# Feed-forward entry by token blocks, and the down products of its last two steps by token block

## The reference, cut to what matters

```python
for l in range(DEPTH):                      # DEPTH = 2
    x = x + token_mixer(rmsnorm(x, ln1_g[l]), ...)
    h = rmsnorm(x, ln2_g[l])
    if l % 2 == 0:
        x = x + (jax.nn.silu(h @ w_gate) * (h @ w_up)) @ w_down   # 1024 -> 2816 -> 1024
    else:
        x = x + moe(h, ...)
return rmsnorm(x, final_g)
```

## Time and profile before

| | |
|---|---|
| median of 3 runs | 1437.19 us (1436.74 to 1437.25) |
| the profiled execution | 1435.53 us, span of the trace 1433.7 us |
| PE busy | 1411.7 us, 98% of the span |
| DVE, ACT, POOL busy | 438.5, 303.6, 135.2 us |
| mean granted TensorE clock | 0.996 of 2.4 GHz |
| chain that ended last | PE 96%, DVE 2%, issue 1%, DMA 1% |

### The profile page before, as it was taken

How to read it: one execution, slowest core, us unless ns; L and a number is a source line. 1 busy time by engine, 2 the same in 40 slices (tenths; PEclk the granted TensorE clock), 3 DMA queues, 4 the chain that set the end, 5 groups by cost and what they waited for, 6 DMA issues and landing times.

```text
span 1433.7 us, 35214 instructions
## 1 busy us (share of the span) xinstructions
PE 1411.7 (98%) x16271; PEld 890.3 (62%) x16271; DVE 438.5 (31%) x719; ACT 303.6 (21%) x426; POOL 135.2 (9%) x164
## 2 busy tenths in 40 slices
PE   9999999999999999999999999999999999999996
PEld 7999999999999984344344344344344344344344
DVE  5775765555776563110110110110110110110122
ACT  5554454444646431000000000000000000000001
POOL 2650000000363000000000000000000000000000
PEclk9999999999999999999999999999999999999999
DMA  9755555666366455999999999999999999999993
GB/s 318 254 177 177 177 167 191 200 214 202 125 208 204 170 194 219 417 420 418 410 420 413 413 421 410 413 420 410 415 419 408 414 421 407 416 420 410 420 421 159
DMA packets 136220, 462.72 MB, mean 323 GB/s; under 512 B 8515, under 2 KB 74849, under 8 KB 121746
## 3 DMA queue, kind: packets, MB, share of 16 engines
q1 hardware_dynamic: 130498, 449.94, 80.8%
q0 software_dynamic: 2448, 7.90, 1.5%
q10 hardware_dynamic: 3136, 2.75, 0.6%
HBM read 455.70 MB, written 4.86 MB: 321 GB/s over the span
## 4 chain that ended last, share of the span: by engine, by line
PE 96%; DVE 2%; issue 1%; DMA 1%; ACT 0%; SPq 0%; POOLq 0%; DVEq 0%; POOL 0%
PE bank L1425 94%; PE bank L1575 1%; DMA mem<-in_w_in_dram 1%; PE bank L1455 0%; DVE w_lo L740 0%; DVE mem L788 0%; DVE mem L782 0%; ACT mem L537 0%; DVE mem L1006 0%; DVE x L804 0%; PE bank L1669 0%; PE bank L1543 0%; PE bank L1606 0%; DVE xt_lo L795 0%; DVE x L1212 0%
## 5 line engine op out<-in xcount | busy, mean ns | idle before, releaser
L1425 PE MATMUL bank<-mem 128*32 128x448 f32 (+2 forms) x11632 | 876.0, 463 | 0.9 <-DVE mem L1219 0.6
L1425 PEld LDWEIGHTS bank<-mem 128*32 128x32 f32 (+1 forms) x11632 | 381.0, 110 | 495.1 <-issue 377.3
L740 DVE TENSOR_TENSOR w_lo<-mem,w_hi 128x1024 fp32r<-128x1024 f32 x178 | 223.1, 1270 | 127.4 <-ACT w_hi L514 126.5
L1265 DVE TENSOR_TENSOR mem<-mem,bank 128x448 f32<-128x448 f32 x48 | 26.9, 616 | 726.1 <-PE bank L1425 726.1
L1425 PE MATMUL bank<-xt_hi,w_hi 128*128 128x256 f32 x864 | 238.8, 276 | 0.0
L1425 PE MATMUL bank<-xt_hi,w_lo 128*128 128x256 f32 x864 | 237.6, 275 | 0.0
L1425 PE MATMUL bank<-xt_lo,w_hi 128*128 128x256 f32 x864 | 237.6, 275 | 0.0
L514 ACT CAST w_hi<-mem 128x1024 fp32r<-128x1024 f32 x178 | 184.4, 1048 | 173.3 <-PE bank L1425 167.9
L1425 PEld LDWEIGHTS bank<-xt_hi,w_hi 128*128 128x128 f32 x864 | 165.8, 192 | 1.3 <-issue 0.7
L1425 PEld LDWEIGHTS bank<-xt_lo,w_hi 128*128 128x128 f32 x864 | 165.8, 192 | 0.3
L1425 PEld LDWEIGHTS bank<-xt_hi,w_lo 128*128 128x128 f32 x864 | 165.9, 192 | 0.0
(11 more groups left out here) (206 smaller groups left out, 722.5 us busy)
## 6 DMA issues: line engine op xcount, KB each, us to landing
mem<-in_eg_dram SPq DMA_DIRECT2D x128, 896.0 KB, 11.0
mem<-in_eu_dram SPq DMA_DIRECT2D x128, 896.0 KB, 10.8
mem<-in_ed_dram SPq DMA_DIRECT2D x112, 1024.0 KB, 13.1
mem<-in_w_in_dram SPq DMA_DIRECT2D x40, 1024.0 KB, 6.4
mem<-in_fg_dram SPq DMA_DIRECT2D x11, 1024.0 KB, 5.3
mem<-in_fu_dram SPq DMA_DIRECT2D x11, 1024.0 KB, 5.3
mem<-in_fd_dram SPq DMA_DIRECT2D x11, 1024.0 KB, 4.9
mem<-in_w_br_dram SPq DMA_DIRECT2D x8, 1024.0 KB, 5.1
```

What stands on the lines that cost most here:

```text
L740: nc.vector.tensor_tensor(w_lo[:, q % H, :], src, w_hi[:, q % H, :].bitcast(F32), ALU.subtract).then_inc(lo_done, 1)
L1265: nc.vector.tensor_tensor(h, h, by_pair(bank[3 + g]), ALU.mult).then_inc(ehf_done, 1)
L1425: return nc.tensor.matmul(out, lhs, rhs, start=first, stop=last, skip_group_check=True)
```

## The change

At the entry, PE computes step 0's gate and up by token block: the normalised tokens become the stationary operand, the weights the moving one, 24 products of 256 columns for each of gate and up and each block (`first_pass`). Gate of block 0 comes ahead of block 1's transposes. Of the 12 zero products 3 stay. The hidden values of step 0 come out with tokens in rows, so four transposes turn them (`first_hidden_turned`) between gate and up of step 1; ACT and DVE work on halves of 256 columns for step 0. On ACT and DVE pieces 60 and 61 are split after the block's last norm operations, piece 59 ahead of them.

At the exit, PE takes the down products of steps 9 and 10 after the gate and up of step 10: block 0 of step 9, block 0 of step 10, then block 1 of both. `y_full` counts each output half. The calls of `until` behind the loop name a number smaller by 2; the loops on ACT and DVE are as they were.

```diff
@@ ACT, feed-forward entry
-                    until(q0 + 2 + H)
-                    act.wait_ge(piece_used, q0 + 2)
-                    nc.scalar.activation(sg[:, :], bank[0][:, :], ACT.Silu).then_inc(sg_done, 1)
-                    until(q0 + 4 + H)
-                    act.wait_ge(hf_done, 1)
-                    nc.scalar.copy(fh_hi[:, 0, :, :], hf[:, 0, :].rearrange("p (k t) -> p k t", k=2)).then_inc(fh_h, 1)
+                    for t in range(TB):
+                        if t == 0:
+                            act.wait_ge(first_gate, 1)
+                        else:
+                            act.wait_ge(piece_used, q0 + 2)
+                        nc.scalar.activation(halves(sg[:, 256 * t:256 * t + 256].unsqueeze(1)),
+                                             unturned(bank[FIRST_BANK[t][0]][:, 0:256]), ACT.Silu).then_inc(first_sg, 1)
+                        until(q0 + 2 * t + 2 + H)
+                    act.wait_ge(first_turned, 1)
+                    nc.scalar.copy(by_block(fh_hi[:, 0, :, :]),
+                                   bank[3][:, :].rearrange("p (k t a) -> p k t a", k=2, t=TB)).then_inc(fh_h, 1)
                     with act.Fori(0, (STEPS - 1) // 2) as r:
...
                     cur[0] = q0 + 4 + 6 * (STEPS - 1) + H
-                    until(q0 + FFN_PIECES + H - 2)
+                    until(q0 + FFN_PIECES + H - 4)
@@ DVE, second layer's first norm
                         if p < 3:
-                            dve.wait_ge(y_full, 1 + (1, 1, 2)[p])
+                            dve.wait_ge(y_full, 2 + p)
@@ PE, feed-forward entry
                 transposes(2 * l + 1, 0, 1)
-                keep_warm(8, bank[UNIT_BANK["wo0"]])
-                transposes(2 * l + 1, 1, 0)
-                transposes(2 * l + 1, 1, 1)
-                keep_warm(4, bank[UNIT_BANK["wo0"]])
+                if l:
...
+                else:
+                    keep_warm(3, bank[UNIT_BANK["wo2"]])
...
+                    def first_pass(t, u):
+
+                        for half in range(2):
+                            pe.wait_ge(tl_done, 4 + 2 * t + half + 1)
+                            w = pair(piece(q0 + 2 * u + half), lambda a: a.rearrange("p (k n) -> p k n", k=4))
+                            for k in range(4):
+                                kk = 4 * half + k
+                                ins = mm3(bank[FIRST_BANK[t][u]][:, 0:256],
+                                          (xt_hi[:, kk, t * P:(t + 1) * P], xt_lo[:, kk, t * P:(t + 1) * P]),
+                                          pair(w, lambda a: turns(a[:, k, :])), kk == 0, kk == KT - 1)
...
-                    up(q0, (None,) * 4, None, ready=4)
+                    first_pass(0, 0)
+                    transposes(1, 1, 0)
+                    transposes(1, 1, 1)
+                    first_pass(0, 1)
+                    first_pass(1, 0)
+                    first_pass(1, 1)
@@ PE, feed-forward exit
-                    pe.wait_ge(fh_l, STEPS)
-                    w = [piece(q0 + FFN_PIECES - 2 + k) for k in range(2)]
                     for t in range(TB):
-                        for half in range(2):
-                            for k in range(2):
-                                ins = down_part(w[k], 0, k, t, half, k == 1)
...
+                        for step_of, s in ((STEPS - 1, 1), (STEPS, 0)):
+                            pe.wait_ge(fh_l, step_of)
+                            w = [piece(q0 + FFN_PIECES - 4 + 2 * (1 - s) + k) for k in range(2)]
+                            for half in range(2):
+                                for k in range(2):
+                                    ins = down_part(w[k], s, k, t, half, s == 0 and k == 1)
+                                    if (t, half) == (1, 1):
+                                        ins.then_inc(piece_used, 1)
+                                if s == 0 and (t, half) != (1, 1):
+                                    ins.then_inc(y_full, 1)
```

More of the change, by code:

```diff
@@ L1041, in _ @@
                 scaled(n, 3)
+                until(base + MIX_PIECES + H - 2)
                 turned_low(n, 2)
@@ L1061, in _ @@
                     q0 = FFN_BASE
-                    until(q0 + 4 + H)
-                    hidden(1, 0, q0 + 4)
+                    for t in range(TB):
+                        dve.wait_ge(first_sg, t + 1)
+                        if t == 0:
+                            dve.wait_ge(first_up, 1)
+                        else:
+                            dve.wait_ge(piece_used, q0 + 4)
+                        cols = slice(256 * t, 256 * t + 256)
+                        nc.vector.tensor_tensor(halves(hf[:, 0:1, cols]), halves(sg[:, cols].unsqueeze(1)),
+                                                unturned(bank[FIRST_BANK[t][1]][:, 0:256]), ALU.mult).then_inc(first_hf, 1)
+                        until(q0 + 2 * t + 2 + H)
+                    dve.wait_ge(first_hf, TB)
+                    dve.wait_ge(fh_h, 1)
+                    nc.vector.tensor_tensor(by_block(fh_lo[:, 0, :, :]),
+                                            bank[3][:, :].rearrange("p (k t a) -> p k t a", k=2, t=TB),
+                                            by_block(fh_hi[:, 0, :, :].bitcast(F32)), ALU.subtract).then_inc(fh_l, 1)
+                    dve.sem_inc(sg_done, 1)
+                    dve.sem_inc(hf_done, 1)
                     with dve.Fori(0, (STEPS - 1) // 2) as r:
@@ L1710, in _, with up @@
                 transposes(2 * l + 1, 0, 1)
[L1711 to L1714 removed]
+                if l:
+                    keep_warm(8, bank[UNIT_BANK["wo0"]])
+                    transposes(2 * l + 1, 1, 0)
+                    transposes(2 * l + 1, 1, 1)
+                    keep_warm(4, bank[UNIT_BANK["wo0"]])
+                else:
+                    keep_warm(3, bank[UNIT_BANK["wo2"]])
                 if l == 0:
                     q0 = FFN_BASE
[L1720 removed]
+                    def first_pass(t, u):
[7 more added lines that the diff above has]
+                                          pair(w, lambda a: turns(a[:, k, :])), kk == 0, kk == KT - 1)
+                            if t == TB - 1:
+                                ins.then_inc(piece_used, 1)
+                        if t == 0:
+                            ins.then_inc((first_gate, first_up)[u], 1)
+                        pe.wait_ge(lo_done, q0 + 2 * u + 2)
+                    def up(q, counts, free, between=None):
                         if free is not None:
                             pe.wait_ge(sg_done, free)
[L1724 removed]
+                        channels(bank[0], q, counts=counts[0:2])
+                        if between is not None:
+                            between()
                         if free is not None:
@@ L1748, in _ @@
                         mm(bank[4 + n][:, :], zeros[:, :], zeros[:, 0:1].to_broadcast([P, 512]), True)
-                    with pe.Fori(0, (STEPS - 1) // 2) as r:
+                    q = q0 + 4
+                    pe.wait_ge(first_sg, TB)
+                    up(q, (None,) * 4, None, first_hidden_turned)
+                    down(q + 4, 0, (None, None), 1)
+                    q = q0 + 10
+                    up(q, (None,) * 4, 2)
+                    down(q + 4, 1, (None, None), 2)
+                    with pe.Fori(1, (STEPS - 1) // 2 - 1) as r:
                         for s in range(2):
```

33 lines of the change are left out of this document (25 added, 8 removed).

## The result

The changed kernel took 1440.03 us (median of 14 runs, 1438.94 to 1440.44), the kernel before 1436.74 us (14 runs, 1435.01 to 1437.32) in the same comparison: a ratio of 1.0025 with a 95% interval of 1.0017 to 1.0033. It is 3.3 us slower; the forecast was +3.6 us and 1440.8 us, with a range of 1437.6 to 1443.4. The profiled execution took 1440.14 us with a span of 1438.3 us, against 1435.53 and 1433.7.

The account below looks back on a forecast made before the run. PE, busy 98% of the span, was taken to bound the kernel. Entry -2.9 and exit +4.7 make +1.8 us, with one clock fall +3.6, put on the median 1437.19: 1440.8 us, range 1437.6 to 1443.4.

Parts of the forecast that it names:

- Entry: Feed-forward entry on PE: step 1 starts 3.3 us earlier, four extra transposes cost 0.36 us; -2.9 us in all.
- The wait for step 10's hidden values: Exit on PE: after 12 instead of 24 step 9 down products, a new wait of 1.95 us, within the exit's +4.7.
- The adds behind two splits: Exit on DVE: first residual add behind splits of pieces 124 and 125, at 364.8 instead of 360.07; exit +4.7 us.
- The clock: Exit on PE: idle times of 1.95 and 2.8 us; one fall to half clock, taken at 1.8 us.
- What I set at nothing: No cost assumed for halved ACT and DVE work at entry, or elsewhere for the mixer's value products and pieces 126 and 127.
- D: Rival, 11%: exit loses nothing, first add 2.4 us or more before the last down product ends; -2.9 us, 1434.3.
- B: Rival, 25%: entry and exit as forecast but no fall of the clock; +1.8 us, 1439.0.
- C: Rival, 17%: a clock fall after each of the two exit gaps; +5.4 us, 1442.6.
- E: Rival, 7%: exit as forecast, no gain at the entry; +4.7 us, 1441.9, with a fall 1443.7.

Follow-up runs that it names:

- entry_only: The changed kernel with the down products of steps 9 and 10 as before the change: 1433.05 us, ratio 0.998, 2.9 us faster than the kernel before.
- hidden_first: splits_behind with step 10's hidden values ahead of piece 123 on ACT and DVE in the last turn: 1433.02 us, ratio 0.9981 to the kernel before.
- splits_behind: The full change with the last ACT and DVE loop turn written out, its last two splits behind block 0's norm: 1434.95 us, ratio 0.9995 to before.
- exit_only: The kernel before with only the new exit (down-product order and y_full counts): 1442.91 us, ratio 1.0047, 7.0 us slower than before.
- fill_gap: The full change with 18 zero products instead of 6 behind the last down product: 1438.71 us, ratio 1.0019 to the kernel before.
- norm_early: hidden_first with block 0 scaled ahead of adds 2 and 3, its transposes ahead of the last 6 down products, zeros and ACT moved: 1432.31 us, ratio 0.997.

## Why the prediction was right

- **Entry, forecast -2.9 us.** Right: 14.12 us instead of 17.37, and 0.36 for the extra transposes; entry_only measured -2.9. The gate's first product came after a wait of 0.29 us for the low part that `tl_done` counts. The halved operations on ACT and DVE stayed under step 1's gate products, as set: the transposes of the hidden values at 200.10 have no wait ahead of them.
- **The wait for step 10's hidden values, forecast 1.95 us.** Right: 24 less 12 products left no cover for a chain that is 4.5 us long. 353.58 is 1.93 us later than 12 products behind 349.06 allow. hidden_first shows which link was long: the cast and split of piece 123 ahead of the hidden product.
- **The adds behind two splits, forecast +4.7 us in all at the exit.** Right: the first add came 4.75 us later. The exit without the fall of the clock is 6.09 - 1.54 = 4.55 us, 0.2 less than the forecast's way gives. The forecast took the 6.17 us from the add to the mixer's product as all on the norm's chain; but before, the scaling stood behind the add that waited for the last product, 3.19 us behind the first add, and now it comes after 2.98. splits_behind and hidden_first took the two losses away one after the other: 1.0 and then 2.9 us below before. That the smaller bounds of `until` did nothing is seen in DVE's rows, where both splits (359.51) still stand ahead of the first add.
- **The clock, forecast one fall at 1.8 us.** Right in kind and place: one fall, behind the longer wait and not directly behind the wait of 1.77 us, in the full change and in exit_only. Its price was 1.5 us (fill_gap). The 1.8 came from the start of the kernel, 4.66 us for 24 products against 2.67, and that row holds more than the fall: in exit_only, whose start is the same code and had no fall, the 24 products and the transposes behind them still stand 3.41 us apart (12.51 to 15.92), before 4.45 (12.60 to 17.05), so by this pair the fall itself cost 1.0 us there. That 1.8 lay so near 1.5 is in part luck. The Trainium skill's rule ("TensorE: Matmul & The Clock Gate", section "Terms") gives 1.5 us from the three full windows at half clock, and 1.7 with the partial ones beside them (0.85 and 0.94). The trace agrees: the measured 1.54 lies between. I had read that page's section "HAM oscillation" as leaving the clock alone through gaps as short as these; the measurement decides otherwise, since a gap of 2.64 us was followed by a fall in two kernels.
- **What I set at nothing and was not.** The sum of the two places is +3.2 us, and the median difference is +3.3; but the two profiled executions differ by 4.6. Between them lie the start (-0.2) and the routing (+1.6), by falls of the clock that come in some executions and not in others. I took the 1.66 us by which the median of before lay above its profiled execution as an offset to add; it was such a group. Both medians stood in their upper groups in this comparison (12 of 14 runs after, 8 of 14 before), and so the two cancelled: that is luck. In the last comparison before had only 8 of 26 runs there. Whether the change itself sends more runs to the upper group these counts don't settle, and why what happened 180 us earlier should matter stays open.
- **The rivals.** D, the other side, is refuted by its own point: the first add started 0.3 us behind the end of the last down product, not 2.4 us or more ahead. It describes splits_behind without the wait, that is hidden_first, and there gave the -2.9 us that it was priced at. B (no fall) is fill_gap: the span of its profiled execution is 1.7 us above that of before, B's price being 1.8. C (two falls at the exit) and E (no gain at the entry) didn't happen.

## What to carry to other kernels

When the order of the bottleneck's work is changed so that results come earlier, look at who reads them in its own list: here the adds stood behind two weight splits that could only start once the reordered products had freed their places, and the scaling behind an add that waits for the last product. The gain came only when the readers' lists were reordered with it (in norm_early DVE's and ACT's, and PE's transposes). Interleaving two steps halves the cover of whatever chain ran under the first; measure that chain first and shorten it (here one split moved behind it). A bound that is lowered changes nothing if the counter that it is compared with is set past it.

## What the runs showed of the hardware

- A wait of PE of 2.64 us was followed by half clock in both kernels that had it, one of 1.77 us directly in none of the four; the stretch of half clock cost 1.5 us, and zero products in the wait kept the clock up (fill_gap). One of 1.85 us, near the end of the kernel before, had full clock in the 48 products behind it (1.00 in the windows from 1421 to 1423). Between 1.85 and 2.64 us nothing was measured.
- The length of the wait does not decide alone: at the kernel's start one of 1.81 us was followed by a fall, the one of 1.85 us was not, nor was one of 1.78 us at the start of exit_only, which is the same code (first row below). The fall cost little there: the next long piece of the chain, 56.48 us of products, started at 26.40 us with it and at 26.17 in the changed kernel without. What took up the rest is a wait of 0.57 us for DVE's split of a piece, which is there in the changed kernel (second row below) and not before: the products behind the transposes start at 17.77, against 17.99 before.

```profile
12.51 0.38 PE L1425 MATMUL bank<-w_hi,xt_hi 128*128 128x256 f32 x1 [1.78 <-DVE xt_lo L795]
```

```profile
17.77 0.35 PE L1458 MATMUL bank<-w_hi,xt_hi 128*128 128x256 f32 x1 [0.57 <-DVE w_lo L756]
```

- In the routing stretch, with waits of 0.35 to 0.6 us and products of 8 columns, the clock falls in some executions and not in others, at a cost of 1.6 us. It splits the runs of one kernel in two groups, and the median jumps by about 1 us with the number in each. With four zero products there, 16 of 17 runs of two kernels lay in the lower group. With differences of 0.2% the groups are to be looked at, not the median alone.
